# The gate sums of a gated recurrence, computed from the gates' high and low parts

## The reference, cut to what matters

```python
def step(state, blk):
    qc, kc, vc, gc = blk
    cum = jnp.cumsum(gc, axis=2)
    rel = jnp.where(lower, cum[:, :, :, None, :] - cum[:, :, None, :, :], -jnp.inf)
    scores = jnp.einsum('bhtd,bhsd,bhtsd->bhts', qc, kc, jnp.exp(rel))
    o = (jnp.einsum('bhts,bhsv->bhtv', scores, vc)
         + jnp.einsum('bhtd,bhdv->bhtv', qc * jnp.exp(cum), state))
    cum_end = cum[:, :, -1:, :]
    state = (jnp.exp(cum_end)[:, :, 0, :, None] * state
             + jnp.einsum('bhsd,bhsv->bhdv', kc * jnp.exp(cum_end - cum), vc))
    return state, o
```

## Time and profile before

| | us |
|---|---|
| median of 3 timed runs | 2212.08 |
| lowest, highest | 2209.62, 2219.95 |
| the profiled execution | 2207.61 |
| its span in the trace | 2205.7 |
| TensorE busy in it | 1956.8 |
| VectorE busy in it | 1235.3 |
| ScalarE busy in it | 911.8 |

### The profile page before, as it was taken

The page is one execution under the profiler, slowest core; times in us unless marked ns, Lnnn a source line. Parts: engine busy times, 40 slices in busy tenths (PEclk is TensorE's granted clock), DMA queues, the critical chain, the costliest instruction groups (busy, mean ns, idle before and its releaser), DMA issues.

```text
span 2205.7 us, 27906 instructions
## 1 busy us (share of the span) xinstructions
PE 1956.8 (89%) x11307; PEld 1623.8 (74%) x11307; DVE 1235.3 (56%) x1928; ACT 911.8 (41%) x1213; POOL 74.3 (3%) x135
## 2 busy tenths in 40 slices
PE   4899878868899999998977887989799889999888
PEld 3678656657677777886864566987699869888777
DVE  3553365663666566355545646785566655455684
ACT  4534422222544444325344125564333435566442
POOL 0100000010100000001000010000100000000010
PEclk8899976669999999998987779999899999999998
DMA  7444200001344443323420015554466545555551
GB/s 261 168 147 153 77 1 1 1 1 58 115 153 153 153 153 115 99 81 131 135 94 1 1 57 164 190 173 153 132 186 191 172 158 160 174 165 169 142 66 39
DMA packets 211453, 261.41 MB, mean 119 GB/s; under 512 B 4657, under 2 KB 173283, under 8 KB 211071
## 3 DMA queue, kind: packets, MB, share of 16 engines
q1 hardware_dynamic: 207690, 248.34, 34.7%
q0 software_dynamic: 3232, 11.15, 2.8%
q10 hardware_dynamic: 405, 0.15, 0.0%
HBM read 258.50 MB, written 1.12 MB: 118 GB/s over the span
## 4 chain that ended last, share of the span: by engine, by line
PE 63%; issue 14%; DVE 12%; ACT 5%; DMA 4%; POOL 1%; SPq 0%; DVEq 0%; ACTq 0%; POOLq 0%
PE acc L627 16%; PE acc L629 15%; PE acc L628 15%; DVE scratch L1791 3%; PE acc L801 2%; PE acc L657 2%; PE acc L658 2%; ACT weights_high L1237 1%; DVE weights_low L1625 1%; PE acc L1096 1%; PE acc L846 1%; PE acc L849 1%; DVE mixer_scratch L1772 1%; PE acc L1072 1%; PE acc L1026 1%
## 5 line engine op out<-in xcount | busy, mean ns | idle before, releaser
L1625 DVE TENSOR_TENSOR weights_low<-weights,weights_high 128x2048 fp32r<-128x2048 f32 x232 | 526.6, 2273 | 590.7 <-ACT weights_high L1237 590.6
L1237 ACT ACTIVATE weights_high<-weights 128x2048 fp32r<-128x2048 f32 x232 | 439.9, 1899 | 613.8 <-DMA weights<-in_w_ada_dram 118.2
L627 PE MATMUL acc<-normed_t_high,weights_high 128*128 128x256 f32 (+1 forms) x1824 | 577.6, 317 | 5.3 <-DVE normed_t_low L1659 2.5
L628 PE MATMUL acc<-normed_t_low,weights_high 128*128 128x256 f32 (+1 forms) x1824 | 565.1, 310 | 0.0
L629 PE MATMUL acc<-normed_t_high,weights_low 128*128 128x256 f32 (+1 forms) x1824 | 563.7, 309 | 0.0
L627 PEld LDWEIGHTS acc<-normed_t_high,weights_high 128*128 128x128 f32 x1824 | 346.6, 190 | 37.1 <-DVE normed_t_low L1659 6.9
L628 PEld LDWEIGHTS acc<-normed_t_low,weights_high 128*128 128x128 f32 x1824 | 344.3, 189 | 22.6 <-issue 3.8
L629 PEld LDWEIGHTS acc<-normed_t_high,weights_low 128*128 128x128 f32 x1824 | 344.4, 189 | 20.8
L627 PE MATMUL acc<-weights_high,normed_t_high 128*128 128x512 f32 (+1 forms) x792 | 315.8, 399 | 28.0 <-DVE normed_t_low L1932 27.9
L629 PE MATMUL acc<-weights_high,normed_t_low 128*128 128x512 f32 (+1 forms) x792 | 310.1, 391 | 0.0
L628 PE MATMUL acc<-weights_low,normed_t_high 128*128 128x512 f32 (+1 forms) x792 | 309.9, 391 | 0.0
(11 more groups left out here) (218 smaller groups left out, 2064.0 us busy)
## 6 DMA issues: line engine op xcount, KB each, us to landing
weights<-in_w_ada_dram SPq DMA_DIRECT2D x48, 1024.0 KB, 5.3
weights<-in_w_up_dram SPq DMA_DIRECT2D x44, 1024.0 KB, 5.9
weights<-in_attn_w_in_dram SPq DMA_DIRECT2D x40, 1024.0 KB, 5.1
weights<-in_conv_w_in_dram SPq DMA_DIRECT2D x32, 1024.0 KB, 5.7
weights<-in_w_in_dram SPq DMA_DIRECT2D x24, 1024.0 KB, 6.4
weights<-in_w_down_dram SPq DMA_DIRECT2D x20, 1024.0 KB, 5.0
weights<-in_w_out_dram SPq DMA_DIRECT2D x8, 1024.0 KB, 5.1
weights<-in_conv_w_out_dram SPq DMA_DIRECT2D x8, 1024.0 KB, 5.1
```

The lines of the kernel that those rows point to most:

```text
L627: pe.matmul(o, ah, bh, start=start, stop=False)
L628: pe.matmul(o, ah, bl, start=False, stop=False)
L1237: act.activation(hi_slot(n)[:, 0:used], slot(n)[:, 0:used], ACT.Copy).then_inc(hi_in.sem, 1)
L1625: dve.tensor_tensor(slot(n, ring_lo)[:, 0:used], slot(n)[:, 0:used], hi_slot(n)[:, 0:used], ALU.subtract).then_inc(lo_in.sem, 1)
```

## The change

The gate sums become two fp32r products that accumulate in the same bank: the high part of the gates with the scan matrices, and their low part with the same matrices, which hold only 0 and 1. ScalarE makes the high part of `GL` by a copy to fp32r, VectorE the low part by a subtraction, tile by tile, with semaphores `g_high` and `g_split`. The parts stand in two of the three `weights_high` buffers, `gate_part(li, 0)` and `gate_part(li, 1)`, those of the second and third piece of `w_out`. So these two pieces are no longer split in `w_in`, but behind the weave, on ScalarE once the last gate sum is read and ahead of `merge_rec`, on VectorE ahead of the split of the merged activations. The scan matrices get their own memory (1 MB on the 128 partitions) and are copied to fp32r once, in place, by ScalarE in layer 0. The matrices for `suf` and a column of ones stay fp32. Of the four `BIAS` tables two now stand over the scan matrices and two in other memory that is free later.

```diff
...
-        top = (nc.sbuf_top - 4 * (SLOTS * SLOT + 2 * KT * 512)) // 32 * 32
+        SCAN = 2 * LEVELS * P
+        top = (nc.sbuf_top - 4 * (SLOTS * SLOT + 2 * KT * 512 + SCAN)) // 32 * 32
...
+        scan = at_top("scan_matrices", SCAN, F32, SLOTS * SLOT + 2 * KT * 512)
+        scan_r = at_top("scan_matrices_single", SCAN, F32R, SLOTS * SLOT + 2 * KT * 512)
...
-        wide = sb("wide_consts", 128 * 4 + 128 + 1024 + 256 + 128 + 512 + 2304)
+        wide = sb("wide_consts", 128 * 4 + 128 + 1024 + 256 + 128 + 512 + 257)
...
+        SUF = part(wide, 256).rearrange("p (d n) -> p d n", d=2)
+        ones = part(wide, 1)
...
-        SM = part(wide, 2304).rearrange("p (d l n) -> p d l n", d=2, l=9)
-        bias_old = wide[:, m0:m0 + 2304].rearrange("p (b g n) -> p b g n", b=3, g=NG)
-        BIAS = [*(bias_old[:, b, :, :] for b in range(3)), ht_b[:, 0:768].rearrange("p (g n) -> p g n", g=NG)]
+        SMR = scan_r[:, :].rearrange("p (d l n) -> p d l n", d=2, l=LEVELS)
+        bias_old = scan[:, 0:1536].rearrange("p (b g n) -> p b g n", b=2, g=NG)
+        BIAS = [*(bias_old[:, b, :, :] for b in range(2)),
+                *(ht_b[:, b:b + 768].rearrange("p (g n) -> p g n", g=NG) for b in (0, 768))]
...
+        def gate_part(li, m):
+
+            return hi_slot(item[("w_out", li, 0, 0)] + 1 + m).rearrange("p (t n) -> p t n", t=NT)
+
...
                         last.then_inc(full, 1)
+                        pe.wait_ge(g_split.sem, g_split.after((li, t)))
                         for p in range(2):
...
                                 o = open_group(("E", li, i, p, hf))
-                                pe.matmul(o[:, :], GL[:, t, d * 256 + p * P:d * 256 + (p + 1) * P],
-                                                SM[:, d, 4 * hf:4 * hf + 4, :], start=True, stop=True).then_inc(full, 1)
+                                cs = slice(d * 256 + p * P, d * 256 + (p + 1) * P)
+                                pe.matmul(o[:, :], gate_part(li, 0)[:, t, cs], SMR[:, d, 4 * hf:4 * hf + 4, :], start=True, stop=False)
+                                pe.matmul(o[:, :], gate_part(li, 1)[:, t, cs], SMR[:, d, 4 * hf:4 * hf + 4, :],
+                                          start=False, stop=True).then_inc(full, 1)
                     if i < 6:
                         o = open_group(("suf", li, i))
-                        pe.matmul(o[:, 0:256], SM[:, d, 8, :], GL[:, t, d * 256:(d + 1) * 256], start=True, stop=True)
-                        end = (P - 1) * (1 - d)
+                        pe.matmul(o[:, 0:256], SUF[:, d, :], GL[:, t, d * 256:(d + 1) * 256], start=True, stop=True)
                         for p in range(2):
                             last = pe.matmul(o[:, 256 + p:257 + p], GL[:, t, d * 256 + p * P:d * 256 + (p + 1) * P],
-                                             SM[:, d, 7, end:end + 1], start=True, stop=True)
+                                             ones, start=True, stop=True)
                         last.then_inc(full, 1)
...
                     pe.wait_ge(*taken_after(("ihgh", li, t)))
+                pe.wait_ge(s_scan, 1)
                 gates(0)
...
-                    sp.dma_start(wide[:, FIRST:], wide_c[:, FIRST:]).then_inc(s_const, 16)
+                    sp.dma_start(wide[:, FIRST:], wide_c[:, FIRST:m0]).then_inc(s_const, 16)
+                    sp.dma_start(scan[:, :], wide_c[:, m0:]).then_inc(s_const, 16)
...
                     pool.wait_ge(b_max.sem, b_max.after((h - NBIAS, 1)))
-                elif h == 3:
+                elif h == 2:
                     pool.wait_ge(full, full_after(("z2", 3)))
...
                 for n, (name, h, _) in enumerate(W_IN):
+                    if (li, name, h) == (0, "ka", 0):
+                        act.wait_ge(s_const, 48)
                     if name in ("qa", "ka"):
...
                         if li == 0:
+                            act.activation(scan_r[:, :], scan[:, :], ACT.Copy).then_inc(s_scan, 1)
                             act.wait_ge(s_mask, 1)
...
                         split_next()
-                    if n < len(W_IN) - 1:
+                    if n < len(W_IN) - 2:
                         split_next()
...
                     act.activation(KTOK[:, t, :], KTOK[:, t, :], ACT.Exp).then_inc(k_ready.sem, 1)
-                split_next()
+                for t in range(NT):
+                    act.wait_ge(g_ready.sem, g_ready.after((li, t)))
+                    act.activation(gate_part(li, 0)[:, t, :], GL[:, t, :], ACT.Copy).then_inc(g_high.sem, 1)
...
                 weave(hgrn(li), attention(li), mixer_steps(li))
+                act.wait_ge(full, full_after(("E", li, 7, 1, 1)))
+                for n in range(2):
+                    split_next()
                 merge_rec(li)
...
                         dve.tensor_tensor(GL[:, t, :], GL[:, t, :], BG[:, t, :], ALU.add).then_inc(g_ready.sem, 1)
-                split_next()
+                for t in range(NT):
+                    dve.wait_ge(g_high.sem, g_high.after((li, t)))
+                    dve.tensor_tensor(gate_part(li, 1)[:, t, :], GL[:, t, :], gate_part(li, 0)[:, t, :], ALU.subtract).then_inc(g_split.sem, 1)
...
                 weave(hgrn(li), attention(li), mixer_steps(li), combine(li))
+                for n in range(2):
+                    split_next()
                 live = range(NT) if li == 0 else range(2, NT)
...
```

More of the change, by code:

```diff
@@ L48, in scan_matrices @@
     u, tau = np.arange(P)[:, None], np.arange(P)[None, :]
-    out = np.zeros((P, 2, 9, P), np.float32)
+    out = np.zeros((P, 2, LEVELS, P), np.float32)
+    rest = np.zeros((P, 2, P), np.float32)
     for level in range(1, LEVELS):
@@ L55, in scan_matrices @@
     out[:, 0, 7], out[:, 1, 7] = u <= tau, u >= tau
-    out[:, 0, 8], out[:, 1, 8] = u > tau, u < tau
-    return out.reshape(P, -1)
+    rest[:, 0], rest[:, 1] = u > tau, u < tau
+    return np.concatenate([rest.reshape(P, -1), np.ones((P, 1), np.float32), out.reshape(P, -1)], axis=1)
 def level_masks():
@@ L1717, in w_in @@
                                 dve.tensor_tensor(X[:, hd, 256:512], X[:, hd, 256:512], rope_t[:, b, :], ALU.add).then_inc(taken_of(key), 1)
-                    for _ in range(len(fill(("w_in", li), n)) + (n < len(W_IN) - 1)):
+                    for _ in range(len(fill(("w_in", li), n)) + (n < len(W_IN) - 2)):
                         split_next()
```

7 lines of the change are left out of this document (5 added, 2 removed).

## The result

The changed kernel takes 2198.81 us (median of 15 executions, 2194.46 to 2203.66), the kernel before 2209.62 us beside it. The ratio is 0.9947, interval 0.9935 to 0.9959: by it 11.7 us less, where 5.0 were forecast. Taken off the 2212.1 us that the forecast started from, that is 2200.4 us: inside the range of 2197 to 2219, but outside the forecast's own 2202 to 2212. The interval excludes a ratio of 1, but not the 0.5% that the prediction called faster: the ratio is a little past it, and the interval reaches across it. The mechanism came as written, the price of the moved splits to a few tenths; the gate sums gave a third more than I had put down for them.

A forecast was written before the change was run, and what follows sets the result against it. The prediction took the recurrences' chain of waits round the engines, with gate sums on the path, as the bound. Terms −12.1 −0.9 + 8.0 = −5.0 us took the median 2212.1 to 2207.0 us; range 2197 to 2219 (8 in 10), own range 2202 to 2212.

The forecast's parts named there:

- the 0.5% that the prediction called faster: Whole kernel: 0.5% (11 us) tells from no change; faster means below 2201, chance 0.17; same 0.76, slower 0.07.
- The rival of fp32r at the fp32 rate: Gate sums: fp32r products run no faster than fp32, 4.7 us more in each of 11 units, 2271 us; chance 2%.
- Their sum, 12.1 us: Gate sums in both recurrences: 5.6 + 2.0 + 1.5 + 3.0 us off the path.
- Pair of units 0 and 1: Layer 0's first two units: TensorE saves 3 us, but VectorE must do unit 0's products first; 1.5 us gained.
- ScalarE is the next bound: Recurrences: exponentials 0.55 us apart limit the gain from faster sums; layer 1's unit 6 gains 0.
- a rival for every unit: Both recurrences: exponentials queue in every unit, only 0.6 us gained in each of 11, 2213 us; chance 17% (ScalarE or VectorE).
- Making the parts, 0.9 us off: Start of the recurrences: copies and subtractions replace a weight split; layer 0 costs 0.4 us, layer 1 gains 1.3.
- The moved splits, 8.0 us: Before the output projections: two late weight splits delay TensorE 3.6 us in layer 0, 4.4 in layer 1; bounds 6 to 11.
- Small pieces at nothing: Constants' transfer cut in two, scan matrices' copy in layer 0's projection, last attention's third bias table: each costs nothing.
- the 3 of the rival: Layer 0 outputs: clock luck puts half of six late stretches at 2.4 GHz, 3 us each, 2198 us; chance 13%.
- all slow before: Layer 0's late output stretches: all ran slow in the wake of VectorE's 7 us of masks; argued against clock luck.
- The case with a clock that stays low: Recurrences and output projections' start: shorter dense stretch keeps TensorE at 1.2 GHz, +11 us, 2223 us; chance 7%.

The follow-up runs named there:

- the run with fp32 sums: The changed kernel with each gate sum one fp32 product again, parts made but not read: 2216.11 us, 1.0032 to the kernel before.
- another order: The changed kernel with the two moved weight splits placed behind the rounding of the merged activations: 2194.74 us (0.9927), later 2191.08 us (0.9915).
- the third table: The kernel before with only the last attention's third bias table started behind the z product: 2210.32 us, 0.9992.
- repeated scores and six small products on resident data: Changed kernel, moved splits behind the rounding, last score group issued five times, six 64-column products before each unit's outputs: 2177.38 us, 0.9853.
- more filling inside the attention steps: The kernel with repeated scores and six small products, plus each attention step's last transpose made six times: 2189.68 us, 0.9900.
- the same kernel unfilled: The changed kernel with its two moved splits behind the rounding, without repeated scores or small products: 2191.08 us, 0.9915 in that job.

## Why the prediction was right or wrong, point by point

- **The gate sums are on the path, and the new ones cost what fp32r products cost elsewhere.** Right: 0.43 and 0.23 us a record, VectorE's wait 1.60 us (1.9 forecast), lap 25.9 (26). The rival of fp32r at the fp32 rate is gone.
- **Their sum, 12.1 us.** This is the term that was mis-sized: 16.4 us in the laps (without unit 4 of layer 1, for which 0.6 had been put down) and 16.1 between the run with fp32 sums and the changed kernel beside it. Pair of units 0 and 1: 1.4 against 1.5, right. Units 2 to 5 of layer 0: 2.2, 1.7, 1.2 and 1.9, together 7.0 against 5.6. The working gave 1.3 to 1.8 a unit, and I took 1.4 "with what the next bound may take of it". ScalarE took little here: its exponentials are 0.49 us apart, not the 0.55 that I read off one group. Units 6 and 7: 1.7 and 1.9, 3.6 against 2.0; I had let 512-key attention steps halve them, and they did not. Single units vary, though: in the other trace of the same kernel units 4 to 7 gave 2.3, 1.3, 1.7 and 1.4, with the same sum to 0.1. In layer 1 unit 5 gave 0.6 (0.5) and unit 6 gave 0.2 (nothing), both right. Unit 7 gave 3.6 where 1.9 stood: 1.5 by its sums and about 2.1 by outputs at the other clock.
- **ScalarE is the next bound.** Right in its place: unit 6 of layer 1 neither gains by shorter sums nor loses by longer ones. As a rival for every unit it failed, since the sums still lead in layer 0; leaving out half of the products gains 0.7 us a unit there on the mean, and nothing in layer 1.
- **Making the parts, 0.9 us off.** About right: layer 1 reaches its first unit 1.7 and 2.9 us earlier in the two traces, where 1.3 and 0.6 for unit 4 were put down. The first gate sum of layer 0 comes 0.5 us earlier, not 0.4 later, but its place varies by 2.5 us over the traces. The run with the moved splits alone reaches the first unit of layer 1 3.1 us earlier, where 2.3 was given as the bound; the 0.8 beyond it lie within what this stretch varies by.
- **The moved splits, 8.0 us.** Right, 3.7 for 3.6 in layer 0 and 4.5 for 4.4 in layer 1, and the waits of 6.30 and 6.62 us are the forecast's "about 7". That nothing covers it was right of the change as it stands; another order covers most of it.
- **Small pieces at nothing.** Right as far as is known: the third table was tested alone, the rest only inside the 7 us of the run with fp32 sums.
- **The sum.** With the measured terms, −16.4 −2.3 (the start of layer 1, mean of two traces) +8.1 = −10.6 us against −5.0, and 9.5 and 11.7 were timed in two jobs. The trace of the changed kernel also has 3.6 us less from the projection of layer 1 to the next one, the second trace of the same kernel 1.5, and 2 us more behind that: such differences come and go with the execution.
- **The clock.** Right that the laps' shift moves it. A hot stretch of outputs is worth 2 us, not the 3 of the rival, and "all slow before" was wrong: units 6 and 7 of layer 0 had part of their outputs at 2.4 GHz, and layer 1 was not looked at. The case with a clock that stays low did not come: the mean granted clock of layer 0's recurrence is 0.72 in the changed kernel and 0.71 before.

With bounds of 1.3 to 1.8 us a unit and no row that showed ScalarE late in the six late units of layer 0, the middle, 1.6, would have been the honest value, and the forecast 2205. Of the 4.6 us from there to 2200.4 the clock in layer 1 is 2.1 and the start of layer 1 about 0.4 (2.3 for 1.9 with unit 4); the rest, 2 us, is less than one execution differs from another. So the size of the gain was in part luck: without the outputs of that one unit it would have been some 2 us smaller.

## What to carry to other kernels

Take a gain a unit from the row of that unit: a next engine takes a share of it only where its own row is late already, and the middle of a worked-out bound should not be shaded for a bound seen elsewhere. When a buffer is lent out, look at what its late refill stands in front of: here two splits of 3.7 us cost 8.1 us ahead of the rounding and about one behind it. In a recurrence that goes round the engines, look at the clock behind TensorE's waits: repeated scores and six small products on resident data in the right place gave as much as the change itself (13.7 us beside 9.5 to 11.7), and more filling inside the attention steps, which are on the path, lost 12 us of it.

## What the runs showed of the hardware that I had not expected

- Twelve half-records of 64 columns, 1.42 us of needless work a unit, and repeated scores in front of them raise the mean granted clock of a recurrence from 0.71 to 0.88 and shorten it by 8 us against the same kernel unfilled (221.6 to 213.8 us). The repeated scores alone raise it to 0.80 and shorten it by 1 us (220.5).
- The level of a short stretch can change by an edit elsewhere and then repeat from trace to trace: the outputs of unit 5 of layer 1 took 2.6 to 2.8 us from the first product to the last in every trace with fp32r sums and 4.56 in every one with fp32 sums.
- Laps cut at the same instructions repeat to 0.2 us in most units between two traces of one kernel (three of layer 0 differ by 0.6 to 1.1), while its executions differ by 6 to 9 us. For terms of one or two microseconds the trace is the better instrument, the timing only for their sum.
